# First norm taken by token rows, padded queries and probabilities cleared under the prompt's attention, and a third buffer for the samples' values

## What is computed

```
hn    = x * rsqrt(mean(x * x) + eps) * norm1_g          # first RMS norm, all 336 tokens
proj  = hn @ w_in                                       # one input projection, 7256 columns
mlstm = matrix memory, 4 heads, of the first columns
attn  = softmax(q k^T * scale + bias, selected keys) v  # 8 heads, prompt and samples
h1    = x + concat(mlstm, attn) @ w_out
y     = h1 + peer(rmsnorm(h1))                          # 128 gathered expert rows per token
```

## Time and profile before

| | us |
|---|---|
| median of three executions | 2598.18 |
| lowest, highest | 2598.0, 2613.66 |
| profiled execution | 2606.02 |
| its span (first to last instruction) | 2604.2 |

### The profile page before, as it was taken

How to read it: one execution, slowest core, us unless ns; L and a number is a source line. 1 busy time by engine, 2 the same in 40 slices (tenths; PEclk the granted TensorE clock), 3 DMA queues, 4 the chain that set the end, 5 groups by cost and what they waited for, 6 DMA issues and landing times.

```text
span 2604.2 us, 20531 instructions
## 1 busy us (share of the span) xinstructions
PE 2224.5 (85%) x7554; PEld 1222.2 (47%) x7554; DVE 1454.1 (56%) x2668; ACT 406.6 (16%) x864; POOL 367.9 (14%) x363
## 2 busy tenths in 40 slices
PE   4999999978899899998999997777777777777776
PEld 3999999745564444343444443323222222222221
DVE  3433333487410166667544457888888855555554
ACT  3322323322201100112000011211111100000000
POOL 0000000000100011212222121222111122122221
PEclk8999999876899999999999999999999999999999
DMA  4445444322368999999999999999999999999997
GB/s 130 156 130 162 137 155 130 111 69 83 104 227 286 330 423 425 376 425 394 416 425 411 427 395 423 416 417 414 427 429 418 426 427 426 428 422 427 429 426 293
DMA packets 159756, 844.82 MB, mean 324 GB/s; under 512 B 9798, under 2 KB 97666, under 8 KB 117146
## 3 DMA queue, kind: packets, MB, share of 16 engines
q0 software_dynamic: 46080, 671.11, 61.1%
q1 hardware_dynamic: 113578, 172.41, 19.7%
HBM read 833.26 MB, written 10.21 MB: 324 GB/s over the span
## 4 chain that ended last, share of the span: by engine, by line
PE 55%; DMA 28%; DVE 10%; issue 4%; ACT 1%; POOL 0%; SPq 0%; DVEq 0%; ACTq 0%; POOLq 0%
DMA rows_in<-in_peer_uv,expert 27%; PE bank L251 20%; PE bank L277 7%; PE bank L1044 5%; PE bank L1045 5%; PE bank L1043 5%; PE bank L264 4%; DVE rows_in L553 3%; PE bank L1208 1%; PE bank L1218 1%; PE bank L1018 1%; DVE diag L528 1%; PE bank L1195 1%; PE bank L1136 1%; PE bank L1124 1%
## 5 line engine op out<-in xcount | busy, mean ns | idle before, releaser
L251 PE MATMUL bank<-rows_in,diag 128*128 128x512 f32 (+1 forms) x2560 | 1180.2, 607 | 266.9 <-DVE diag L528 266.9
L553 DVE CUSTOM_DVE_ANT_0 rows_in<-rows_in,x2n 128x2048 f32<-128x2048 f32 x320 | 733.4, 2292 | 518.2 <-DMA rows_in<-in_peer_uv,expert 517.9
L251 PEld LDWEIGHTS bank<-rows_in,diag 128*128 128x128 f32 (+1 forms) x2560 | 447.6, 181 | 981.3 <-issue 536.4
L459 POOL DMA_INDIRECT rows_in<-in_peer_uv,expert x320 | 352.6, 1102 | 1494.1 <-PE bank L251 1307.0
L1043 PE MATMUL bank<-xnh,wh 128*128 128x336 f32 (+2 forms) x928 | 293.3, 316 | 20.3 <-DVE wl L1451 20.3
L361 ACT ACTIVATE dots<-dots 128x1 f32<-128x1 f32 x320 | 64.9, 203 | 1504.1 <-DVE dots L553 1504.1
L1044 PE MATMUL bank<-xnl,wh 128*128 128x336 f32 (+2 forms) x928 | 291.6, 314 | 0.0
L1045 PE MATMUL bank<-xnh,wl 128*128 128x336 f32 (+2 forms) x928 | 291.5, 314 | 0.0
L1451 DVE TENSOR_TENSOR wl<-wring,wh 128x2048 fp32r<-128x2048 f32 (+1 forms) x58 | 132.0, 2278 | 233.2 <-ACT wh L1273 233.2
L1043 PEld LDWEIGHTS bank<-xnh,wh 128*128 128x128 f32 (+1 forms) x928 | 174.9, 188 | 22.1 <-issue 20.8
L1044 PEld LDWEIGHTS bank<-xnl,wh 128*128 128x128 f32 (+1 forms) x928 | 174.9, 188 | 1.3
(11 more groups left out here) (294 smaller groups left out, 1380.9 us busy)
## 6 DMA issues: line engine op xcount, KB each, us to landing
wring<-in_w_in SPq DMA_DIRECT2D x28, 2048.0 KB, 8.3
wk<-in_w_out SPq DMA_DIRECT2D x64, 512.0 KB, 10.1
wk<-in_peer_wq SPq DMA_DIRECT2D x64, 512.0 KB, 8.5
kT<-in_keys_t SPq DMA_DIRECT2D x16, 512.0 KB, 6.5
vpage<-in_cache_v SPq DMA_DIRECT2D x16, 512.0 KB, 4.5
rows_in<-in_peer_uv,expert POOLq DMA_INDIRECT x320
C<-in_state_C SPq DMA_DIRECT2D x4, 1024.0 KB, 5.8
out_C_sample<-C SPq DMA_DIRECT2D x4, 1024.0 KB, 4.4
```

The lines of the kernel that those rows point to most:

```text
L251: mm = pe.matmul(accs[t][d][0:w, :], diag[r % ND][:, 0:w], rows_in[r % NG][:, D + 512 * d:D + 512 * d + 512], start=False, stop=(j == ROUN ...
L459: nc.gpsimd.indirect_dma_start(out=rows_in[r % NG][:], out_offset=None, in_=UV_DR, in_offset=bass.IndirectOffsetOnAxis(ap=ids[:, j:j + 1], ...
L553: nc.vector.tensor_tensor_reduce(u, u, x2n[t][:], 1.0, 0.0, ALU.mult, ALU.add, dots[t % 2][:, j:j + 1]).then_inc(S["dot_done"], 1)
```

## The change

The first norm is taken on the token rows before the transposes: ScalarE squares a tile of `xnat` with an accumulated sum, the reciprocal root is one column per tile, and VectorE scales the tile in place by it and by the gain vector `g1`, which a DMA spreads over all partitions. TensorE transposes the scaled tile; ScalarE rounds the banks straight to `xnh`, VectorE subtracts from the same banks to get `xnl`. `xT`, `xnT`, `rnorm` and `norm_sum` are gone. Each x tile has its own semaphore. The first two weight blocks are issued ahead of the small loads; the gain columns and the bias products move behind the second tile of the projection. `logit` and `probT` move to other addresses, so that `qpad` and `pz` no longer overlap them, and POOL's wait for ("aO", 1, 7) is dropped. `vpage` gets a third buffer, value loads wait one pass less, and SP waits for the last logits before it loads output weights.

```diff
-    jobs += [("gcols",), ("bias", 0), ("bias", 1), ("norm1",)]
-    early = [(key, n % 8) for n, key in enumerate(jobs)] + [(("bt", h), 4 + h % 4) for h in range(AH)]
+    early = [(key, n % 8) for n, key in enumerate(jobs)] + [(("gcols",), 4), (("bias", 0), 5), (("bias", 1), 6)] + [(("bt", h), 4 + h % 4) for h in range(AH)]
...
-        logit = [at(f"logit{s}", o_, [P, TP]) for s, o_ in enumerate((AV + 5472, AV + 6560, ML))]
-        probT = [at(f"probT{s}", AV + 7648 + s * 1536, [P, 3, P]) for s in range(2)]
+        logit = [at(f"logit{s}", PR + 1088 * s, [P, TP]) for s in range(3)]
+        probT = [at(f"probT{s}", PR + 3264 + s * 1536, [P, 3, P]) for s in range(2)]
...
-        pz = at("pz", NR + 16896, [P, 2, AH, 2 * TS - ST])
-        vpage = [at(f"vpage{s}", PR + s * 8192, [P, 2, AH * DH]) for s in range(2)]
+        pz = at("pz", NR + 8448, [P, 2, AH, 2 * TS - ST])
+        vpage = [at(f"vpage{s}", o_, [P, 2, AH * DH]) for s, o_ in enumerate((PR, PR + 8192, SI))]
...
+            sp.dma_start(xnat[0:META, 0, :], mt).then_inc(S["x_in0"], 16)
+            sp.dma_start(xnat[META:P, 0, :], xp[0:P - META]).then_inc(S["x_in0"], 16)
+            g = a["norm1_g"][0]
+            sp.dma_start(g1[:], bass.AP(tensor=g.tensor, offset=g.offset, ap=[[0, P], [1, D]])).then_inc(S["g1_in"], 16)
+            sp.dma_start(xnat[:, 1, :], xp[P - META:2 * P - META]).then_inc(S["x_in1"], 16)
+            sp.dma_start(xnat[0:META, 2, :], xp[2 * P - META:SEQ]).then_inc(S["x_in2"], 16)
+            sp.dma_start(xnat[META:META + TS, 2, :], xs).then_inc(S["x_in2"], 16)
+            for b in range(2):
+                load_block(b)
...
-            load_values(0)
-            load_values(1)
+            for b in range(3):
+                load_values(b)
             take(sp, ("sL", 0))
             load_keys(2)
             for b in range(2, SB):
                 if b + 1 < SB:
                     take(sp, ("sL", b - 1))
                     load_keys(b + 1)
-                sp.wait_ge(S["sO_done"], b - 1)
-                load_values(b)
+                if b >= 3:
+                    sp.wait_ge(S["sO_done"], b - 2)
+                    load_values(b)
+            take(sp, ("sL", SB - 1))
...
             for i, (_, w) in enumerate(XTILES):
-                pe.wait_ge(S["x_in"], 80)
+                pe.wait_ge(S["xn_done"], i + 1)
                 for q in range(4):
                     b = open_bank(("x", i, q))
...
                 weight_tile(n)
+                if n == 1:
+                    b = open_bank(("gcols",))
+                    pe.wait_ge(S["small_in"], 16 * SMALL_LOADS)
+                    close(flip(b[:, 0:56], grow[:], 56))
+                    pe.wait_ge(S["bhot_in"], 16)
+                    for c in range(2):
+                        b = open_bank(("bias", c))
+                        close(pe.matmul(b[0:AH, 0:RW // 2], relb[:], bhot[:, c * (RW // 2):(c + 1) * (RW // 2)], start=True, stop=True))
...
+            def row_square(i):
+
+                w = XTILES[i][1]
+                act.wait_ge(S[f"x_in{i}"], (32, 16, 32)[i])
+                nc.scalar.activation(squares[0:w, :], xnat[0:w, i, :], ACT.Square, accum_out=rms1[0:w, i:i + 1]).then_inc(S["square"], 1)
+                act.wait_ge(S["mean_done"], i + 1)
+                nc.scalar.activation(rms1[0:w, i:i + 1], rms1[0:w, i:i + 1], ACT.Sqrt).then_inc(S["rms_done"], 1)
+
+            def token_high(i):
+
+                c, w = XTILES[i]
+                for q in range(4):
+                    b = take(act, ("x", i, q))
+                    nc.scalar.copy(xnh[:, 4 * q:4 * q + 4, c:c + w], b[:, 0:4 * w].rearrange("p (n w) -> p n w", n=4)).then_inc(S["xnh_done"], 1)
...
+            row_square(0)
+            row_square(1)
+            token_high(0)
+            row_square(2)
+            token_high(1)
+            token_high(2)
...
             nc.gpsimd.tensor_copy(kiT[:, :, PAST:KS], ikT[:, TP:T].rearrange("p (b t) -> p b t", t=ST)).then_inc(S["iqz_done"], 1)
-            take(pool, ("aO", 1, AH - 1))
             pool.wait_ge(S["v_sent"], 64)
             nc.gpsimd.memset(pz[:], 0.0).then_inc(S["pz_zero"], 1)
...
+            def row_scale(i):
+
+                w = XTILES[i][1]
+                r, s = rms1[0:w, i:i + 1], rms1[0:w, 3 + i:4 + i]
+                dve.wait_ge(S["square"], i + 1)
+                nc.vector.tensor_scalar(r, r, 1.0 / D, EPS, ALU.mult, ALU.add).then_inc(S["mean_done"], 1)
+                dve.wait_ge(S["rms_done"], i + 1)
+                link(nc.vector.reciprocal(s, r))
+                dve.wait_ge(S["g1_in"], 16)
+                nc.vector.scalar_tensor_tensor(xnat[0:w, i, :], xnat[0:w, i, :], s, g1[0:w, :], ALU.mult, ALU.mult).then_inc(S["xn_done"], 1)
+
+            def token_low(i):
+
+                c, w = XTILES[i]
+                for q in range(4):
+                    b = take(dve, ("x", i, q))
+                    dve.wait_ge(S["xnh_done"], 4 * i + q + 1)
+                    give(nc.vector.tensor_tensor(xnl[:, 4 * q:4 * q + 4, c:c + w], b[:, 0:4 * w].rearrange("p (n w) -> p n w", n=4),
+                                                 xnh[:, 4 * q:4 * q + 4, c:c + w].bitcast(F32), ALU.subtract), ("x", i, q))
...
+            row_scale(0)
+            row_scale(1)
+            token_low(0)
+            row_scale(2)
+            token_low(1)
+            token_low(2)
```

More of the change, by code:

```diff
@@ L1018, in flip @@
                 return pe.transpose(out_, in_, ident[0:rows, 0:rows])
-            def norm_sum(key, turn, width, squares_):
-                b = open_bank(key)
-                for c in range(KC):
-                    pe.wait_ge(S["square"], KC * turn + c + 1)
-                    mm = pe.matmul(b[:, 0:width], ones, squares_[c % 2][:, 0:width], start=(c == 0), stop=(c == KC - 1))
-                    if c < KC - 1:
-                        mm.then_inc(S["square_used"], 1)
-                close(mm)
             def weight_tile(n):
@@ L1055, in _ @@
                     close(mm)
-            pe.wait_ge(S["small_in"], 16 * SMALL_LOADS)
-            close(flip(open_bank(("gcols",))[:, 0:56], grow[:], 56))
-            pe.wait_ge(S["bhot_in"], 16)
-            for n in range(2):
-                b = open_bank(("bias", n))
-                close(pe.matmul(b[0:AH, 0:RW // 2], relb[:], bhot[:, n * (RW // 2):(n + 1) * (RW // 2)], start=True, stop=True))
-            norm_sum(("norm1",), 0, T, squares)
-            banks_idle(pe, ("norm1",), range(4))
-            pe.wait_ge(S["xnl_done"], KC)
+            for i in range(3):
+                for q in range(4):
+                    evacuated(pe, ("x", i, q))
             for n in range(TILES):
@@ L1252, in link @@
                 act.wait_ge(S["act_step"], steps[0])
-            def square_all(turn, src, squares_, ready):
-                for c in range(KC):
-                    ready(c)
-                    if c >= 2:
-                        act.wait_ge(S["square_used"], (KC - 1) * turn + c - 1)
-                    nc.scalar.activation(squares_[c % 2][:, 0:src.shape[2]], src[:, c, :], ACT.Square).then_inc(S["square"], 1)
-            def root(key, turn, width):
-                evacuated(act, key)
-                nc.scalar.activation(rnorm[:, 0:width], rnorm[:, 0:width], ACT.Sqrt).then_inc(S["rnorm_sqrt"], 1)
+            def row_square(i):
[9 more added lines that the diff above has]
+                    nc.scalar.copy(xnh[:, 4 * q:4 * q + 4, c:c + w], b[:, 0:4 * w].rearrange("p (n w) -> p n w", n=4)).then_inc(S["xnh_done"], 1)
             def high(n):
@@ L1505, in _ @@
                 if n == 2:
+                    b = take(dve, ("gcols",))
+                    give(nc.vector.tensor_copy(gcol[:], b[:, 0:56]), ("gcols",))
                     for c in range(2):
```

63 lines of the change are left out of this document (11 added, 52 removed).

## The result

| | before | after |
|---|---|---|
| median of four executions each, us | 2605.92 | 2580.61 |
| lowest to highest | 2598.0 to 2619.24 | 2569.9 to 2590.78 |
| profiled execution, its span | 2606.02, 2604.2 | 2590.78, 2588.2 |

The ratio is 0.9895, with a 95% interval of 0.9861 to 0.9929: faster by 1.05%, some 27 us, where 30.9 were forecast. The time itself, 2580.6, lies 13.3 us above the forecast 2567.3 and 3.6 above the end of its range. Two separate things are in that: of the gain 5.6 us are missing (30.9 less the medians' 25.3), and 7.7 us are the base, since the kernel before took 2605.9 in the comparison and not the 2598.2 from which I subtracted. Whether the gain reaches the 1% on which the chances were set is not decided: 0.99 lies inside the interval.

A forecast was written before the change was run, and what follows sets the result against it. A latency chain bounds the start, TensorE the middle, DMA the end. Norm and projection net 21.9 us plus parts 2 and 3 at 9.0 make 30.9 off the median 2598.2: 2567.3 us, range 2559 to 2577.

The forecast's parts named there:

- The norm: Start, ahead of the projection: norm in natural layout brings the first product from 55.2 to 32.0 us, 23.2 us off.
- The projection: Input projection: moved gain columns' transpose and bias products add 1.3 us; the same 6 us at half clock.
- The prompt's attention: POOL clears and fills under the prompt's attention: costs VectorE nothing, at worst 7.6 us.
- longer than 61: Sign of a wrong forecast: prompt attention longer than 61 us would mean POOL in VectorE's way.
- Parts 2 and 3: Samples' attention: early clearing and filling by POOL (5.0 us) and third value buffer (4.0 us), together 9.0 us off.
- part 3: Samples' attention, third value buffer: keys issued earlier, all 3.6 us of key waits go; taken 4.0, bounds 2 and 4.5.
- The base: Whole kernel: gain subtracted from median 2598.2; the profiled 2606.0 lay 7.8 us above, most likely in the gathering part.
- B: Samples' part: waits take back nearly all, clock falls and sample 2's keys are late; gain 25, 2573 us; chance 0.18.
- C: Start: norm's chain longer, x1 or gain vector late; first product near 36.5, gain 26, 2572 us; chance 0.17.
- D: More than forecast: x1 at 13 us, no clock fall while waiting; gain 36, 2562 us; chance 0.15.
- E: Projection: full clock granted late after only transposes; gain used up at 68 us of half clock, slower beyond; chance 0.03.
- The rule that I had weighed: Start: transposes don't count for full clock, so the last tile's could run at half, 1 us less gain; not taken.

The follow-up runs named there:

- e6: The kernel after with the second token tile's load issued ahead of the gain vector's; 2580.74 us.
- a1: The kernel after, unedited, profiled a second time; 2584.96 us.
- e3: The kernel after with two value buffers and the old order of waits on SP, clearing still early; 2579.11 us.
- e5: The kernel after with POOL's two clearings cut into twelve pieces, each awaited before the next; 2587.19 us.
- e4: The kernel after with the first three heads' probability scalings written as scalar_tensor_tensor in place of tensor_scalar; 2582.95 us.
- b1: The kernel before, unedited, profiled a second time; 2605.46 us.
- b2: The kernel before, unedited, profiled a third time; 2605.82 us.
- e1: The kernel after with POOL's wait and two value buffers put back, leaving only the new norm and the new addresses; 2593.28 us.
- e10: e9 with the third sample's keys loaded ahead of the values and its logits ahead of the first transposes; median 2567.55 us, ratio 0.9838 against the kernel before.
- e7: The kernel after with small weights and constants issued ahead of the big weight blocks, as before the change; 2576.41 us.
- e9: The kernel after with e4's scaling form and the first two samples' logits multiplied ahead of the masks, key and value loads reordered; 2577.21 us.
- e2: The kernel after with POOL's wait for the prompt attention's last output put back, so clearing is late again; 2577.95 us.

## Why the prediction was right or wrong, point by point

- **The norm** (right, in part by luck). First product forecast for 32.0, at 31.35 in the profiled execution and at 31.8 in the mean of ten kernels with this start; against 55.0 before that is 23.2 us, as forecast (24.0 in the two of the table). The steps stand where they were put: x1 at 13.90 for 14.2, VectorE nearly gapless from 16.6 for 16.9, the small weights in at 21.4 for 22, the last token tile scaled to 24.2 for 24.9. "Each us by which x1 comes later is one us" holds to a hundredth within either group of e6's comparison. Luck was in the transposes. "About 3.4 us" for sixteen and "about 2.2" for the last tile, taken as prices at the full clock, lie at those of half clock (3.42 and 2.40 us measured; at full clock 1.96 and 1.33). The last tile did run at half clock in the kernel after. What the sentence left out is the gain vector, which takes over as soon as x1 is moved ahead of it (e6).
- **The projection** (right). 1.3 us were to be added, with the same 6 us at half clock. Eight of the eleven kernels with the new norm, a1 among them, have 5.0 to 6.1 us of half clock there (6.1 before) and a projection that is 1.0 to 1.8 us longer, 1.2 in the mean. The kernel after, e3 and e5 have 3 us of it and are 0 to 0.6 longer. So the +0.5 of the table, from one profile of each sort, understates what the moved products cost.
- **The prompt's attention** (wrong, the step that failed). "What POOL's work could cost VectorE: ... so nothing, at worst the 7.6 us themselves if VectorE stood still for them." It cost 5.0 us, two thirds of the bound I had named and then dropped. The evidence was MAX8, MATCH_REPLACE8 and their like beside the clearing; the prompt's attention has another instruction, a scaling of one tensor by a column, and that one stands still (e4, e5). A row of one form was taken for an engine. The sign I named for it did show: from the start of the prompt's attention to the first sample logits it was 65.0 us (592.51 to 657.50), with "longer than 61" as the mark. Without these 5.0 us the time would have been 2575.6, inside the range; without the base's 7.7 it would have been too (2572.9). The Trainium skill (SBUF — State Buffer, SBUF: two separate sides) says that one pair of SBUF ports is shared by VectorE and POOL as an exclusive lock: a VectorE operation in a two-port mode (tensor_scalar is among those that can be in one) and a POOL operation shut each other out, while one with two SBUF inputs contends only with a POOL operation that reads SBUF, which a memset doesn't. This case agrees on both counts: 5.36 us for 0.36 in the one form, 0.44 and 0.50 us in the forms with two tensors (e4). I had not weighed this rule; priced by the two clearings of the earlier trace rows such a rival would have cost up to 5.6 us.
- **Parts 2 and 3 in the samples' part** (right in mechanism, 1.0 short). 9.0 forecast, 8.0 measured. The limit did move from POOL to the selection; the clock did fall while TensorE waited (5.46 us for 3.78), as I thought more likely. Two terms of part 3 were mis-sized. "All 3.6 us go" counted the key waits of one profile; b1 and b2, the same kernel, have 2.3 us of them, and this is most of why their stretch is 79.3 and 78.9 and not 80.9. And "up to 1 us of new wait; I take 0" was 1.18 in one profile of the kernel after and nothing in the other, so "no wait for keys from the third sample on" held in one of two. Against the 80.9 of the profile that the forecast was read from, the gain is 8.5 and 9.8. The clearing stands at 597.8 to 603.3 and not near 622 to 629: these were times of the kernel before, 24 us later.
- **The base** (wrong, and the larger share of the 13.3 us). The forecast was hung on 2598.2, the median of three, two of which lay at the low end of what this kernel does: sixteen more of its executions, in the comparison and beside the experiments, lie between 2597.5 and 2622.9, and the median in the comparison was 2605.9 (2605.8 over all nineteen). The profiled execution (2606.0) was the better base; I put its 7.8 us down to the gathering part, and its expert part was in fact the shortest of three (1704.1), while its mLSTM's was the longest (133.4, clock 0.80). From 2605.9 the forecast would be 2575.0.
- **The rivals.** None happened: the samples' gain was not taken back (B), x1 was in at 13.9, in the variants at up to 16.4, and not at 17 (C) or 13 (D), the clock fell during the wait (against D), and half clock at the start of the projection lasted 6.1 us at most (against E). The gain came out near B's 25 us by another road, one with no rival.

## What to carry to other kernels

Before work is moved to an engine that idles beside another, take the other's rows in that very stretch, form by form: one instruction that waits is enough when each step hangs on it. If it must run there, change the form of the few instructions beside it, or cut the work into pieces. A wait that is taken away uncovers the next one within microseconds, here the selection, then the probabilities, then the keys; look up all three before the edit, and put the loads in the order of their use. Forecast from as many executions as there are, and judge small steps by stretches.

## What the runs showed that was not expected

- **A VectorE scaling beside POOL's memsets.** tensor_scalar of 128x272 with a column took 0.36 us alone, 5.36 beside two memsets back to back, and 0.36, 0.66 and 0.80 beside memsets of 0.49 to 0.61 us that are each awaited. It began in the first memset and did not get its turn when the second followed (599.40, before the first one's end at 599.46): the wait lasts over the whole row of them. Short POOL copies did not hold up a tensor_scalar of 64x264, as the timeline of e1 shows (0.29 us, as in the kernel after with nothing beside it). There the copies were the ones to wait: of the eight, six took 0.24 us, the one that began beside this tensor_scalar 0.36, and the next, beside a tensor_tensor, 0.52:

```profile
657.80 1.88 POOL L1408 COPY qpad<-projT 128x64 f32<-128x64 f32 x8
658.12 0.29 DVE L1692 TENSOR_SCALAR keepS<-scoreS 64x264 f32<-64x264 f32 x1
```

- **The clock in transposes, and its price.** The new lead-in is nothing but transposes, and the clock rose and fell within it. The timeline of the kernel after, then that of a1:

```profile
14.15 3.42 PE L1022 MATMUL bank<-c,xnat 128*128 128x128 f32 x16 [14.15 <-DVE xnat L1435]
18.97 1.96 PE L1022 MATMUL bank<-c,xnat 128*128 128x128 f32 x16 [1.39 <-DVE xnat L1435]
```

```profile
19.07 3.60 PE L1022 MATMUL bank<-c,xnat 128*128 128x128 f32 x16 [0.90 <-DVE xnat L1435]
24.34 1.33 PE L1022 MATMUL bank<-c,xnat 80*128 80x80 f32 x16 [1.67 <-DVE xnat L1435]
```

  The same sixteen transposes take 3.4 to 3.7 us or 1.96, the two levels of the clock. In the kernel after the second tile ran at full clock; TensorE then idled 3.30 us, was granted 0.50 from 24.0 on, and the last tile's sixteen took 2.40 us (first timeline). In a1 the second tile still ran at half clock and the last one at full, in 1.33 us. Half clock in the last tile: the kernel after, e4, e5 and e10 (which never rose to full before the projection); full: a1, e1, e3, e6, e7, e9, and e2 nearly (1.47). Idling does not sort them: it was 3.3 us in the kernel after, e4 and e5, 1.6 to 1.9 in most others, but 1.58 in e10 and 3.52 in e6. The profile's view prints a granted clock of 1.00 for any time ahead of the first change that it recorded (17.2 us in the kernel after, 22.5 in a1, 37.8 in e10), and that is no reading. Twenty-four of the 48 transposes in the kernel before ran at half clock too (a bank of four every 0.85 us up to 20 us, every 0.44 or less after 20.7), where the prediction took 1.00 for all of them; and the same 32 transposes that keep TensorE busy for 5.38 us in the kernel after keep it busy for 7.25 in a1, both under a printed 1.00:

```profile
14.00:24.00 10.00, 5.38 (x32) 4.94 (x32) 7.46 (x11) 8.05 (x14) 0.00 (x0) 1.00 1.06 314
```

```profile
14.00:24.00 10.00, 7.25 (x32) 6.55 (x32) 7.73 (x11) 8.33 (x14) 0.00 (x0) 1.00 1.05 310
```

  The last tile's clock is the difference between the 17.45 and 16.60 us from x1 to the first product: ScalarE's highs wait for the transposes, and VectorE then waits 0.76 us for ScalarE ahead of the weights' low half, as the first timeline shows; in a1 it does not wait there. The rule that I had weighed (the Trainium skill, TensorE: Matmul & The Clock Gate, Part 4: PE-mode transpose) says that the full clock does not engage for transposes. Here it did, in ten of eleven kernels, ahead of any other product. What it cost is near what I had put on it, 1 us: 0.85 us in four of ten kernels and nothing in six.
- **A 1 MB load that spreads one row of 8 KB over 128 partitions** landed after 8.2 us, about as a load of 1 MB of rows did (8.9 in the earlier trace rows).
